# Attention of a two-layer encoder step: prompt keys, values and bias rows in SBUF, one-pass bias and masks, the streams' loads in order

## The reference, cut to what matters

```python
def _fox_attention(q, k, v, logf):
    cum = jnp.cumsum(logf.astype(jnp.float32), axis=1).transpose(0, 2, 1)
    ...
        s = jnp.einsum('bqhd,bkhd->bhqk', q[:, start:stop], k[:, :kend]).astype(jnp.float32) * scale
        bias = cum[:, :, off + start:off + stop, None] - cum[:, :, None, :kend]
        mask = kpos[None, :] <= qpos[:, None]
        p = jax.nn.softmax(jnp.where(mask, s + bias, -jnp.inf), axis=-1)
        outs.append(jnp.einsum('bhqk,bkhd->bqhd', p.astype(v.dtype), v[:, :kend]))
```

## Time and profile before

| what | value |
|---|---|
| three runs, median | 1713.01 us (1710.75 to 1714.33) |
| the profiled execution, and its span | 1714.5 us, 1712.7 us |
| TensorE busy | 1633.2 us, 95% |
| VectorE, ScalarE, GpSimd busy | 773.6, 599.2, 263.6 us |
| chain that ended last, TensorE's share | 87% |
| DMA | 301.58 MB, mean 176 GB/s |

### The profile page before, as it was taken

One profiled execution on the slowest core, in us unless ns is written; L12 is line 12 of the kernel. 1 busy time (PEld: TensorE's weight loads), 2 busy tenths in 40 slices (PEclk: granted clock), 3 DMA queues, 4 the chain that ended last, 5 costly groups with the idle time before them and its releaser, 6 DMA issues.

```text
span 1712.7 us, 31703 instructions
## 1 busy us (share of the span) xinstructions
PE 1633.2 (95%) x12630; PEld 1512.1 (88%) x12630; DVE 773.6 (45%) x1158; ACT 599.2 (35%) x877; POOL 263.6 (15%) x286
## 2 busy tenths in 40 slices
PE   5999999999899999999999999999889899999996
PEld 4999999988689999989788999999856589999996
DVE  3443345642486334334652333345434565433444
ACT  2433333432344333322443343433423334333332
POOL 1200011230253000022220000022411053000121
PEclk9999999999899999999999999999989999999998
DMA  8544556588843555565435543453553942333441
GB/s 348 185 166 165 183 184 233 183 247 233 315 175 112 183 172 166 187 231 178 151 128 208 170 163 123 169 210 128 205 173 117 329 146 74 122 130 129 134 137 48
DMA packets 88250, 301.58 MB, mean 176 GB/s; under 512 B 11048, under 2 KB 15816, under 8 KB 86736
## 3 DMA queue, kind: packets, MB, share of 16 engines
q1 hardware_dynamic: 85088, 294.96, 50.0%
q10 hardware_dynamic: 3072, 5.35, 1.2%
HBM read 283.57 MB, written 6.00 MB: 169 GB/s over the span
## 4 chain that ended last, share of the span: by engine, by line
PE 87%; DVE 4%; DMA 3%; POOL 2%; issue 2%; ACT 1%; SPq 1%; ACTq 0%; DVEq 0%; POOLq 0%
PE bank L1368 70%; PE bank L1376 5%; PE bank L1399 3%; PE bank L1517 2%; DMA land<-ADA 1%; PE bank L1572 1%; DVE z L1007 1%; DMA araw<-ADA 1%; PE bank L1594 1%; DMA gapL<-ADA 1%; PE bank L1657 1%; PE bank L1599 1%; DVE z L1014 1%; DVE hL L1091 1%; PE bank L1625 1%
## 5 line engine op out<-in xcount | busy, mean ns | idle before, releaser
L1368 PE MATMUL bank<-hH,wH 128*128 128x384 f32 x1536 | 525.3, 342 | 10.6 <-DVE hL L1091 6.3
L1368 PE MATMUL bank<-hH,wL 128*128 128x384 f32 x1536 | 517.5, 337 | 0.0
L1368 PE MATMUL bank<-hL,wH 128*128 128x384 f32 x1536 | 517.4, 337 | 0.0
L733 ACT ACTIVATE wH<-raw 128x1024 fp32r<-128x1024 f32 x328 | 345.0, 1057 | 488.5 <-PE bank L1368 477.2
L972 DVE TENSOR_TENSOR wL<-raw,wH 128x1024 fp32r<-128x1024 f32 x328 | 413.2, 1284 | 195.9 <-ACT wH L733 192.9
L1368 PEld LDWEIGHTS bank<-hH,wH 128*128 128x128 f32 x1536 | 291.0, 189 | 25.3 <-issue 16.6
L1368 PEld LDWEIGHTS bank<-hL,wH 128*128 128x128 f32 x1536 | 291.3, 190 | 0.4
L1368 PEld LDWEIGHTS bank<-hH,wL 128*128 128x128 f32 x1536 | 291.1, 189 | 0.0
L1139 DVE TENSOR_TENSOR tmp<-sg,bank 128x384 f32<-128x384 f32 x88 | 48.8, 554 | 451.1 <-PE bank L1368 429.4
L1368 PE MATMUL bank<-hidH,wH 128*128 128x384 f32 x704 | 238.6, 339 | 0.0
L1368 PE MATMUL bank<-hidL,wH 128*128 128x384 f32 x704 | 235.9, 335 | 0.0
(11 more groups left out here) (180 smaller groups left out, 1534.7 us busy)
## 6 DMA issues: line engine op xcount, KB each, us to landing
raw<-W SPq DMA_DIRECT2D x328, 512.0 KB, 4.0
araw<-ADA SPq DMA_DIRECT2D x92, 512.0 KB, 5.5
land<-ADA SPq DMA_DIRECT2D x16, 512.0 KB, 14.8
gapE<-ADA SPq DMA_DIRECT2D x16, 512.0 KB, 6.3
KTb<-kt_d SPq DMA_DIRECT2D x8, 1024.0 KB, 6.0
Vb<-v_d SPq DMA_DIRECT2D x8, 1024.0 KB, 5.1
gapH<-ADA SPq DMA_DIRECT2D x12, 512.0 KB, 5.5
gapL<-ADA SPq DMA_DIRECT2D x12, 512.0 KB, 6.1
```

The costliest lines, as they stand in the source:

```text
L733: a.activation(wH[:, slot, :], raw[:, slot, :], ACT.Copy).then_inc(w_hi, 1)
L1368: op = mm(out, tile_w(w, slot, k), m[:, k0 + k, :], start=start and k == 0 and q == 0, stop=stop and k == nk - 1 and q == 2)
```

## The change

- **Forget sums.** One tile `lfA` holds all sums. ScalarE rounds it (`lfH`), VectorE takes the difference (`lfL`), and both go to DRAM (`nc_d`). Before the query units all come back as 32 rows (`ncR`), and ScalarE copies them to float32r (`ncA`) ahead of its first query. Bias and masks are then one float32r pass, with constants (`conR`) rounded at the start.
- **Prompt.** All keys (`KA`) and values (`VA`) are loaded once. Scores take 64 rows of `q32` and `KA` directly, without `qP`; there is a bias matmul for each head, and the second head's product waits for the first's (`qk_mm`).
- **Queries.** The second four units use banks 4 to 7; the scores of jobs 0 and 1 stand between them. ScalarE doesn't wait for POOL's residual there.
- **Order.** All prompt jobs, then all stream jobs, written out and not in loops. The turn has a bank of its own, so that transposes don't wait for copies out of it.
- **SyncE.** Stream loads are keys b, values b, keys b + 1, values b + 1, with the same two buffers and the same conditions.
- **adaLN.** Blocks 28 to 33 all belong to the third FFN and its gap (five in the first loop, one in the second); none is left in the attention.

```diff
-        FFN_ADA = [(0, 5, 1), (15, 5, 2), (25, 3, 0), (36, 0, 0)]
-        FFN_GAP = [(6, 7, 8), (22, 23, 24), (28, 29, 30), ()]
+        FFN_ADA = [(0, 5, 1), (15, 5, 2), (25, 5, 1), (36, 0, 0)]
+        FFN_GAP = [(6, 7, 8), (22, 23, 24), (31, 32, 33), ()]
...
+        def pairs_free(b):
+
+            return AT["s", b - 2, 1] + 1
...
             sp.wait_ge(ncum_done, NG)
-            sp.dma_start(ncs_d, lfS[:]).then_inc(nc_out, 16)
-            sp.dma_start(ncp_d, lfP[:]).then_inc(nc_out, 16)
-            sp.dma_start(lf_o, lf_n[:]).then_inc(nc_out, 16)
+            sp.dma_start(lf_o, lf_n[:]).then_inc(lfo_done, 16)
+            sp.wait_ge(nch_done, 1)
+            sp.dma_start(nc_d[0], lfH[:].bitcast(F32)).then_inc(nc_out, 16)
+            sp.wait_ge(ncl_done, 1)
+            sp.dma_start(nc_d[1], lfL[:].bitcast(F32)).then_inc(nc_out, 16)
             w_units(U_V + RING, 2 * RING)
...
+            sp.dma_start(ncR[:], nc_d.rearrange("a h n -> (a h) n")).then_inc(nc_in, 16)
+            sp.dma_start(KA[:], kT_o[:, :, 0:SEQ]).then_inc(ka_in, 16)
+            sp.dma_start(VA[:], v_o[0:SEQ, :].rearrange("(t p) n -> p t n", p=P)).then_inc(va_in, 16)
             sp.dma_start(Kn[:], kT_o[:, :, SEQ:T]).then_inc(kn_in, 16)
+            stream_k(0)
             w_units(U_O, RING)
...
+            stream_k(1)
+            sp.wait_ge(w_used, U_O)
+            stream_v(0)
+            stream_v(1)
+            for b in range(2, DB):
+                sp.wait_ge(s_mm, pairs_free(b))
+                stream_k(b)
+                sp.wait_ge(pv_mm, pairs_free(b))
+                stream_v(b)
             w_units(U_O + RING, RING)
...
-            act.wait_ge(nc_out, 48)
+            act.wait_ge(ncum_done, NG)
+            a.activation(lfH[:], lfA[:], ACT.Copy).then_inc(nch_done, 1)
+            act.wait_ge(ncl_done, 1)
             split_h(M_S3, 4, kv32, hH)
...
-            act.wait_ge(xa_done, 5 * KT)
-            with act.Fori(0, 2) as i:
...
+            act.wait_ge(nc_in, 16)
+            a.activation(ncA[:], ncR[:], ACT.Copy).then_inc(ncr_done, 1)
+
+            def query(k):
...
             modulate(4)
+            dve.wait_ge(nch_done, 1)
+            v.tensor_tensor(lfL[:], lfA[:], lfH[:].bitcast(F32), ALU.subtract).then_inc(ncl_done, 1)
+            dve.wait_ge(lfo_done, 16)
             rest_h(M_S3, kv32, hH, hL)
...
                 if kind == "p":
-                    if j % 2 == 0:
-                        pe.wait_ge(kp_in[s], 32 * i + 32)
-                        pe.wait_ge(qp_done, 4 * i + 2 * s + 2)
-
-
-                    mm(S[:, 0:2 * w], con[0:1, C_ONE:C_ONE + P], ncP[0:1, s, :, 0:w], start=True, stop=False)
-                    qt = j % 2
                     for hh in range(2):
-                        c0 = hh * w
-                        mm(S[:, c0 + w - P:c0 + w], ident, con[:, C_MP:C_MP + P], start=False, stop=False)
-                        op = mm(S[:, c0:c0 + w], qP[:, s, hh, P * qt:P * qt + P], KP[:, s, 0:w],
-                                start=False, stop=hh == 1)
+                        rows, out = slice(HD * hh, HD * hh + HD), S[:, hh * w:hh * w + w]
+                        mm(out, conR[0:2 * H, R_HEAD + 2 * i + hh:R_HEAD + 2 * i + hh + 1].to_broadcast([2 * H, P]),
+                           ncA[:, DB * NK:DB * NK + w], start=True, stop=False)
+                        mm(out[:, w - P:w], conR[:, 0:P], conR[:, R_MP:R_MP + P], start=False, stop=False)
+                        if hh == 1:
+                            pe.wait_ge(qk_mm, 2 * i + half + 1)
+                        op = mm(out, q32[rows, i, P * half:P * half + P], KA[rows, i, 0:w], start=False, stop=True)
+                        if hh == 0:
+                            op.then_inc(qk_mm, 1)
...
+                    mm(S[:, 0:NK], conR[0:2 * H, R_SELH + P * half:R_SELH + P * half + P],
+                       ncA[:, NK * i:NK * i + NK], start=True, stop=False)
+                    mm(S[:, PAST:NK], conR[:, 0:P], conR[:, R_MS:R_MS + DS], start=False, stop=False)
...
+            for j in range(RING):
+                unit(U_Q + RING + j, j, bank[RING + j][:, 0:T], hH, hL)
+                if j == 1:
+                    pe.wait_ge(ncr_done, 1)
+                    pe.wait_ge(ka_in, 16)
+                    scores(0)
+                elif j == 2:
+                    scores(1)
+            pe.wait_ge(q_done, KT)
```

More of the change, by code:

```diff
@@ new lines, in _ @@
+            for k in range(KT - 2):
+                query(k)
+            soft(0)
+            query(KT - 2)
+            soft(1)
+            query(KT - 1)
+            for n in range(2, NJ + 2):
+                if n < NJ:
+                    soft(n)
+                evac_t(n - 2)
+            act.wait_ge(turned, 2 * DB)
+            for k0, nk in PARTS:
+                if k0 == 4:
+                    act.wait_ge(pv_free, NJ)
+                a.activation(hH[:, k0:k0 + nk, :], z[:, k0:k0 + nk, :], ACT.Copy).then_inc(hh_done, nk)
@@ L1279, in _, with row_max @@
             ffn(2)
-            for n in range(U_Q + RING, U_O + RING):
-                refill(n, n % RING)
-            def row_max(kind, i, j):
-                slot, w = j % 4, width(kind, j)
-                dve.wait_ge(s_mm, job(kind, i, j) + 1)
+            def row_max(n):
+                (kind, i, half), slot = JOBS[n], n % 4
+                w = width(kind, half)
+                dve.wait_ge(s_mm, n + 1)
                 if kind == "p":
@@ L1341, in _ @@
-            dve.wait_ge(xa_done, 5 * KT)
-            body("p", 0)
-            with dve.Fori(1, 4) as i:
-                body("p", i)
-            body("s", 0)
-            with dve.Fori(1, 4) as i:
-                body("s", i)
-            body("s", 4, scores=False)
+                op.then_inc(turned, 1)
+            for n in range(U_Q + RING, U_O + 2):
+                refill(n, n % RING)
+            row_max(0)
+            refill(U_O + 2, 2)
+            row_max(1)
+            norm(0)
@@ L1349, in _ @@
+            refill(U_O + 3, 3)
+            dve.wait_ge(xa_done, 5 * KT)
+            for n in range(2, NJ + 4):
+                if n < NJ:
+                    row_max(n)
+                if n <= NJ:
+                    norm(n - 1)
+                if 3 <= n < NJ + 3:
+                    out(n - 3)
+                if n >= 4 and JOBS[n - 4][0] == "s":
+                    out_stream(n - 4)
             rest_h(M_O, z, hH, hL)
@@ L1483, in ffn @@
                 stats(FFN_LN[fi], FFN_GAP[fi])
[L1485 removed]
+            pe.wait_ge(con_in, 32)
             pe.wait_ge(cact_ok, 1)
@@ new lines, in _ @@
+            for j in range(RING):
[7 more added lines that the diff above has]
+            pe.wait_ge(q_done, KT)
+            for n in range(2, NJ + 4):
+                if n < NJ:
+                    if n == 4:
+                        pe.wait_ge(kn_in, 16)
+                    scores(n)
+                if n < NJ + 2:
+                    transposes(n - 2)
+                if 3 <= n < NJ + 3:
+                    if n == 3:
+                        pe.wait_ge(va_in, 16)
+                    values(n - 3)
+                if n >= 4 and JOBS[n - 4][0] == "s":
+                    turn(n - 4)
```

418 lines of the change are left out of this document (148 added, 270 removed).

## The result

The changed kernel takes 1777.4 us (median of 4 runs, 1775.99 to 1779.69) against 1712.4 us for the kernel before: 1.0389 times as long, 95% interval 1.0363 to 1.0416. The direction was forecast, the size wasn't: +65 us where +9 was said, and outside the range of 1706 to 1733.

The account below looks back on a forecast made before the run. TensorE, busy nearly everywhere, was taken as the bound. Prompt half -33.2, adaLN pieces +8.2, forget sums +5.2, query stage +1.2 and streams +27.3 sum to +8.7, giving 1721.7 us from the 1713.0 median; range 1706 to 1733.

Parts of the forecast that it names:

- Prompt jobs: Attention's prompt half: one-pass bias and masks, a pair 4.7 us at full clock, 35.2 instead of 68.4 us: -33.2.
- -32.0: Forecast from the attention input's last rounding to the first stream product: prompt half -33.2 and query stage +1.2.
- (c): Prompt jobs: narrow single passes cost as much as double ones; pair 5.4, half 41, result 1727.5 us; chance 0.20.
- lower bound of a wide job: Prompt half: a wide job's scores with covered weight loads, 1.31 us; 1.7 was taken.
- upper bounds: Prompt half: narrow and wide jobs' scores with about 0.1 us uncovered load at each of six matmuls, 1.55 and 2.05.
- Query stage: Before the prompt jobs: the residual wait goes, but sums returning from DRAM and ScalarE's copy delay the first query: +1.2 us.
- Forget sums and pieces: K and V stage: rounding and low parts delay second-half weights, +5.2; twelve adaLN pieces in the third FFN, +8.2 us.
- Streams: Stream half: SP's order makes TensorE wait about 5.1 us for keys five times, then half clock: +27.3 (+16 to +31).
- (a): Stream half: loads stay hidden, so it only gains 8.8 us; sum -27.4, result 1685.6 us; chance 0.11.
- (b): Stream half: waits happen but the clock stays full; sum -1.9, result 1711 us; chance 0.14.
- side sum for two loads: Stream loads: the skill's DMA formula gives 7.1 us for both where rows have 7.9; result would be 1717.6.

Follow-up runs that it names:

- 7: Kernel with 128-row products, one-pass bias and masks and early keys (1697.39 us), plus the wait between heads: 1703.82 us; with wait and 64-row products: 1742.0 us.
- 10: Kernel with 128-row products, one-pass bias and masks and early keys (1697.39 us), ScalarE's bias-row copy moved behind the fourth query: 1692.38 us, 0.9881 of the kernel before.
- 3: Kernel before with only its twelve adaLN pieces moved to the third FFN: 1695.2 us against 1707.0.
- 1: Changed kernel with only SyncE's order of stream loads put back, keys one block ahead of values: 1738.96 us against 1709.1 for the kernel before.
- 9: Kernel with 128-row products, one-pass bias and masks and early keys (1697.39 us), given the changed kernel's order of stream loads: 1736.15 us.
- 2: Kernel before with only the order of stream loads changed to keys b, values b, keys b+1: 1752.29 us against 1707.0.
- 6: Changed kernel, early keys, no idle moment, four forms: 64 rows one-pass 1736.05, two-pass 1796.86; 128 rows one-pass 1697.39, two-pass (fourth) 1713.86 us.
- 8: Kernel before with adaLN pieces in the third FFN (1695.2 us), its products made 64 rows with a wait between heads: 1774.95 us.
- 5: Changed kernel with three more unread one-pass 128x256 matmuls ahead of each prompt job: 1788.59 us against 1707.0 for the kernel before.
- 4: Changed kernel with parts taken back: two-pass bias and masks 1803.79 us; 128-row padded products, no wait between heads, 1776.08 us; both parts 1769.25 us.

## Why the prediction was wrong, point by point

**Prompt jobs: the step that failed.** I wrote of the prompt half "Its waits for adaLN pieces and the half clock go with it", and took full clock for every job. The waits went, the half clock came back without a wait. The nearest I had was the earlier trace rows, where half clock follows idleness, and I carried that over as if nothing else could lower it. What the runs give of the 39.9 us between -32.0 and +7.9:
- 64 rows instead of 128 cost 30.9 us from the last rounding to the first stream product (101.5 against 70.6 in the two kernels of 7). Of that 8 x 0.77 = 6.2 are uncovered weight loads (1.85 + 2.39 against 1.47 + 2.00 a pair), and the other 24.7 are the clock.
- Even padded, the jobs take 5.28 a pair and not 4.7: scores 1.47 and 2.00 where I took 1.2 and 1.7. Eight pairs: 4.6. The rival (c) had sized the pair at 5.4 and was nearer. With 64 rows at full clock it would be 4.24 + 1.80 = 6.0, above the 5.89 of before, so this form is no shorter than the old one even at full clock.
- The query stage, from the last rounding to the first prompt job behind the query units, took 34.6 us, of which 4.2 are the two score jobs within it. The rest is 30.3 where it was 28.0 before: +2.3, where +1.2 was said. That is 1.1.
- The changed kernel is 3.4 us longer here than the 64-row kernel of 7 (104.9 against 101.5). They differ in the order of jobs 2 and 3, in the idle 0.58 us and in where the queries are read from, and no run takes that apart.

These make 30.9 + 4.6 + 1.1 + 3.4 = 40.0.

The sizes of the jobs had two slips. I wrote that nothing in the trace is a one-pass matmul under 384 columns, but the turn of the earlier trace rows is one of 128 columns, with 0.26 from its start to the next; the bias came at 0.25 and not at 0.11 to 0.16. And in a wide job the bias runs over 256 columns, one pass of which is 0.21 by the same rows; I gave it the size of the narrow one, and it took 0.31 (1275.79 to 1276.10). So the lower bound of a wide job was 1.5 and not 1.31. The upper bounds, 1.55 and 2.05, were too low for 64 rows (1.85 and 2.39).

In the kernel of 10 this stretch is 64.5 us where it was 97.0: -32.5, beside the forecast of -32.0. That it comes so near is luck: the jobs cost 4.6 more than I took, and the query stage, with the copy moved, some 5.5 less (23.7 against 28.0, where +1.2 was said).

**Query stage.** The copy ahead of the first query was seen, and took 2.23 us (2.3 to 2.5 said). The sums took longer to come back: their read was issued at 1231.91 and the copy began at 1235.74, 3.8 us later where I had 2.7. TensorE then stood 4.4 us for the weights that are rounded behind the first query, and worked at 0.50 behind that; the kernel before stood 2.33 us for the same weights, held up by POOL's residual, which is why the stage lost only 2.3. What I didn't see is that the copy could stand elsewhere: moved, it gave 6.1 us (10).

**Forget sums and pieces.** Together +16.6 for +13.4. The twelve pieces cost 9.5 in the kernel of 3, within 7.0 to 9.5 (8.2 taken). Of the other 7.1, 1.8 lie ahead of the change: the last scan began at 880.25, before at 878.49, and in the kernels of 1 to 10 that come from the changed one it began anywhere between 877.2 and 883.5, though none of them changes the work up to there. From the end of that scan to the last rounding it is 348.9 us against 334.1, which is 14.8, and without the pieces 5.3, where 5.2 was taken:

```profile
880.25 0.65 DVE L1229 TENSOR_TENSOR_SCAN lfA<-par,lf_n 16x256 f32<-16x256 f32 x1
...
880.93 2.24 ACT L844 ACTIVATE lfH<-lfA 16x2432 fp32r<-16x2432 f32 x1 [7.06 <-DVE lfA L1229]
886.10 3.15 ACT L734 ACTIVATE hH<-kv 128x384 fp32r<-128x384 f32 x5 [2.93 <-DVE lfL L1233]
891.49 1.06 ACT L685 ACTIVATE wH<-raw 128x1024 fp32r<-128x1024 f32 x1 [2.25 <-DMA raw<-W]
```

The mechanism is as told: the rounding (2.24 us), then the low parts (2.67), then the split, 5.2 behind the scan's end where I had 5.4. SyncE let the weights go at 886.44, and TensorE waited 4.3 us for them, where about 3 was said. No run took this part back by itself, so its 5.3 us are read from the marks alone.

**Streams.** The mechanism was right to the row. SyncE's issues in the changed kernel, one block of five:

```profile
1366.02 0.37 SPq L515 DMA_DIRECT2D Vb<-v_d  x1
1366.44 0.47 SPq L516 DMA_DIRECT2D Vn<-v_o  x1
1366.95 0.42 SPq L512 DMA_DIRECT2D KTb<-kt_d  x1
```

The landing of the five key loads, among the rows of their tile:

```profile
DMA to landing us min/median/max: 6.8/7.1/8.4
```

Keys are issued 0.9 us behind values and land 8.0 us behind the values' issue, as taken from the earlier trace rows. The jobs after a wait begin at 1361.54, 1373.98, 1386.49, 1400.35 and 1413.26: four cycles of 12.4, 12.5, 13.9 and 12.9 where 12.5 was said, 1.7 us more in all. Two ends were wrong. The first waited job came 27.7 us into the half and not 19.0, because the jobs before it ran at the half clock that the prompt half had left (second row by stretch above: 0.50). Behind the last one it was 18.9 and not 15.9, for half clock too. 8.7 + 1.7 + 3.0 = 13.4, and the error is 40.4 - 27.3 = 13.1. But the waits themselves (18.9) were smaller than five times 5.1, and the clock's part larger than 2 us a block; the length of the cycle is set by the queue, and hides how it divides.

The term was also too low by itself. With full clock from the prompt half on, the stream half is 92.2 us (9), which is 35.2 above before and outside my bound of 31; the other 5.2 of the 13.1 are the half clock that the prompt half left. Of the 7.9 over +27.3, 3.1 are the order, which costs 39.2 there (92.2 against 53.0) where my sum had 36.1 (27.3 + 8.8). I had left the clock to return within a cycle, and in 2 it is 0.50 for 76 us, with 62.76 us of work in them. The other 4.8 are a gain that came out smaller: with the early keys the half is 4.0 us shorter than before where I had 8.8, for a job at full clock takes 2.80 us and not 2.69 (16 x 0.11 = 1.8), and 2.9 us of short waits for keys and new values come in.

**Rivals.** (a), streams hidden, didn't come true, but with the order of before it does: 53.0 us for the half, where it had 48.8. (b), full clock through the waits, is excluded by 2 and 9. (c) was near with its pair of 5.4, but not with its reason: at full clock a one-pass bias and mask of 128 columns take 0.25 and 0.17, the two-pass ones of the fourth kernel of 6 0.42 and 0.32. What no rival had was a fall of the clock with TensorE never idle. It was the greatest term of all (24.7 us by 7), and the earlier trace rows, where half clock stands behind a wait, gave no hint of it.

The Trainium skill, page "TensorE: Matmul & The Clock Gate", section "Why this matters for your kernels", advises no idle gaps between bursts of matmuls to avoid drops of the clock. The falls in the streams agree (2 and 9: waits up to 6.0 and 6.2 us, then 0.50). The fall in the prompt half doesn't: 56.00 us of work in 56.00 at 0.50. The measurement decides: to be busy isn't enough here. The prediction's side sum for two loads, 7.1 us, comes to 6.8 from the terms given with it; the runs have 8.0.

What stays open: what the hardware counts. The runs show that the 64-row form brings the clock down, and that the 128-row form keeps it up but, once down behind a wait of 3.6 us, brings it back late (two passes, after 32 us) or not at all within the prompt half (one pass). Whether it is the rows in use, the key data that the other 64 rows carry, or the weight loads that lie open beside a 64-row matmul, no run here tells apart, as they come together. Open loads by themselves are not enough: in the padded kernels the mask's load behind the 32-row bias lies open too (both start at 1273.66), and the clock holds.

## What to carry to other kernels

A matmul over half of the rows isn't a cheaper one, and zero rows aren't waste: padded to 128 rows the products took less time at full clock and kept the clock there, and that was worth 31 us here. Read the granted clock beside the busy time before a cause is named, and price a wait with the work at half clock that follows it: 16 us of waits cost 43 (2). In a queue shared by two kinds of loads, put first the one that is needed first, even if its buffer has been free for long.

## What the runs showed of the hardware that was not expected

- The granted clock falls to 0.50 with TensorE busy without a break, within some 10 us of a row of jobs with 64-row products (between 1271 and 1274 in the kernel of 7, whose jobs began at 1264.2), and stays there as long as they last: 54 to 90 us (7, 8).
- At half clock three more one-pass matmuls of 128 rows a job don't raise it (72 us at 0.50 in 5). The same jobs with 128-row products run at 1.00 without a break for over 30 us if they begin at full clock, and at 0.50 for 32 us (two passes) or at least 62 us (one pass) if they begin behind a wait of 3.6 us (6 against 4).
- The weight load of a 64-row product behind a 128-row mask lies open: it starts with its own matmul (1264.71), where that of a 128-row product starts 0.06 us ahead of it (1273.77); from mask to next bias it is 0.68 us in place of 0.53.
- ScalarE rounds 2432 columns in 2.24 us on 16 partitions and in 2.23 on 32.
